# The last four steps of both output projections, instead of the last two, run block by block of tokens

## The reference

```
# first block
mix = concatenate([rmsnorm(o_a), rmsnorm(o_b)]) @ w_out          # first output projection
x = x + rmsnorm(mix, post_mix_g)
h = rmsnorm(x, pre_ffn_g)
u = causal_dwconv(h @ w_up, conv_w, conv_b); gate, val = split(u)
x = x + rmsnorm((gelu(gate) * val) @ w_down, post_ffn_g)
# second block, with shifts, scales and gates from a modulation network of c
x = x + g_a * (concatenate([attn, pool]) @ w_out_2)              # second output projection
hm = modulate(rms_norm(x, norm_mlp_w), sh_m, sc_m)
x = x + g_m * (square(relu(hm @ w_mlp_up)) @ w_mlp_down)
return rms_norm(x, final_norm_w)
```

## Time and profile before

| | |
|---|---|
| median of 3 runs | 2138.3 us (2136.77 to 2139.04) |
| profiled execution | 2135.51 us, its span 2133.8 us |
| mean granted TensorE clock | 0.996 of full |
| PE busy | 2100.0 us (98%) |
| DVE busy | 1552.3 us (73%) |
| ACT busy | 1091.9 us (51%) |

### The profile page before, as it was taken

One profiled execution on the slowest core, in us unless ns is written; L12 is line 12 of the kernel. 1 busy time (PEld: TensorE's weight loads), 2 busy tenths in 40 slices (PEclk: granted clock), 3 DMA queues, 4 the chain that ended last, 5 costly groups with the idle time before them and its releaser, 6 DMA issues.

```text
span 2133.8 us, 33198 instructions
## 1 busy us (share of the span) xinstructions
PE 2100.0 (98%) x10453; PEld 1750.3 (82%) x10453; DVE 1552.3 (73%) x2201; ACT 1091.9 (51%) x1499; POOL 120.3 (6%) x223
## 2 busy tenths in 40 slices
PE   6999999999999999999999999999999999999998
PEld 5888788888888888888888867888888888888886
DVE  4998889888988888768787554566656656655766
ACT  5445654655545554355587465464434434443444
POOL 1110000000001000100000000010000000000000
PEclk9999999999999999999999999999999999999999
DMA  9988168888899788987856542657667766766763
GB/s 342 305 287 268 60 227 266 271 271 283 276 305 302 264 277 297 296 261 247 258 176 197 182 138 100 188 172 253 208 197 233 221 192 225 237 193 213 226 208 109
DMA packets 282338, 492.35 MB, mean 231 GB/s; under 512 B 26385, under 2 KB 120849, under 8 KB 280657
## 3 DMA queue, kind: packets, MB, share of 16 engines
q1 hardware_dynamic: 251648, 373.52, 53.9%
q0 software_dynamic: 30256, 116.84, 16.5%
q10 hardware_dynamic: 288, 0.11, 0.0%
HBM read 488.24 MB, written 2.13 MB: 230 GB/s over the span
## 4 chain that ended last, share of the span: by engine, by line
PE 97%; ACT 1%; DVE 1%; issue 1%; SPq 0%; DMA 0%; ACTq 0%; DVEq 0%
PE G L1977 21%; PE G L1979 21%; PE G L1978 21%; PE G L1992 6%; PE T L1992 6%; PE T L1994 3%; PE G L1994 3%; PE T L1979 3%; PE T L1978 3%; PE T L1977 3%; PE T L2140 1%; PE T L2216 1%; PE T L2365 1%; PE T L2026 1%; PE G L2347 1%; PE G L2120 1%
## 5 line engine op out<-in xcount | busy, mean ns | idle before, releaser
L1135 DVE TENSOR_TENSOR w_lo<-raw,w_hi 128x1024 fp32r<-128x1024 f32 (+1 forms) x704 | 850.3, 1218 | 442.3 <-ACT w_hi L588 440.2
L588 ACT ACTIVATE w_hi<-raw 128x1024 fp32r<-128x1024 f32 (+1 forms) x704 | 740.9, 1055 | 810.9 <-PE G L1979 525.3
L1977 PE MATMUL G<-w_hi,h_both 128*128 128x512 f32 (+1 forms) x1144 | 448.4, 392 | 14.8 <-issue 8.5
L1979 PE MATMUL G<-w_hi,h_both 128*128 128x512 f32 (+1 forms) x1144 | 444.2, 388 | 0.0
L1978 PE MATMUL G<-w_lo,h_both 128*128 128x512 f32 (+1 forms) x1144 | 444.2, 388 | 0.0
L1977 PE MATMUL G<-w_hi,a_hi 128*128 128x512 f32 x880 | 344.8, 392 | 1.1 <-ACT pooled L1053 0.7
L1979 PE MATMUL G<-w_hi,a_lo 128*128 128x512 f32 x880 | 343.1, 390 | 0.0
L1978 PE MATMUL G<-w_lo,a_hi 128*128 128x512 f32 x880 | 343.0, 390 | 0.0
L1977 PEld LDWEIGHTS G<-w_hi,h_both 128*128 128x128 f32 x1144 | 215.8, 189 | 60.0 <-issue 15.7
L1979 PEld LDWEIGHTS G<-w_hi,h_both 128*128 128x128 f32 x1144 | 215.9, 189 | 44.2
L1978 PEld LDWEIGHTS G<-w_lo,h_both 128*128 128x128 f32 x1144 | 216.0, 189 | 42.2
(11 more groups left out here) (294 smaller groups left out, 2140.5 us busy)
## 6 DMA issues: line engine op xcount, KB each, us to landing
ada_w<-in_w_ada_turned POOLq DMA_DIRECT2D x192, 512.0 KB, 5.7
raw<-in_w_up SPq DMA_DIRECT2D x352, 256.0 KB, 4.8
raw<-in_w_mlp_up SPq DMA_DIRECT2D x256, 256.0 KB, 2.8
raw<-in_w_mlp_down SPq DMA_DIRECT2D x256, 256.0 KB, 3.3
raw<-in_w_in SPq DMA_DIRECT2D x224, 256.0 KB, 4.0
raw<-in_w_down SPq DMA_DIRECT2D x176, 256.0 KB, 4.9
raw<-in_w_out SPq DMA_DIRECT2D x128, 256.0 KB, 3.6
raw<-in_w_in SPq DMA_DIRECT2D x16, 136.0 KB, 3.3
```

The source lines that it names most:

```text
L588: act.activation(w_hi[:, s % 4, :, 0:width], raw[:, s % 8, :, 0:width], ACT.Copy).then_inc(hi_ready, 1)
L1135: dve.tensor_tensor(w_lo[:, s % 4, :, 0:width], raw[:, s % 8, :, 0:width], w_hi[:, s % 4, :, 0:width].bitcast(F32), ALU.subtract).then_inc ...
L1977: pe.matmul(out, ah, wh, start=f, stop=False)
L1979: mm = pe.matmul(out, al, wh, start=False, stop=l)
```

## The change

In both output projections, steps 28 to 31 go by `last_steps` (its argument `n` is 4 in place of the default 2), and `steps` ends after step 27. PE does steps 28 to 31 for block 0, 24 matmuls, and then steps 28 to 31 for block 1. The matmuls are the same ones, in another order. Nothing changes on ACT, DVE, POOL or SP.

```diff
@@ first output projection
-        steps(s0 + 24, 0, 6, 1, H, r, e0 + 4)
-        last_steps(s0 + 30, H[0], 12, r)
+        steps(s0 + 24, 0, 4, 1, H, r, e0 + 4)
+        last_steps(s0 + 28, H[0], 8, r, 4)
@@ second output projection
-        steps(s0 + 24, 0, 6, 1, A, r, e0 + 4)
-        last_steps(s0 + 30, A[0], 12, r)
+        steps(s0 + 24, 0, 4, 1, A, r, e0 + 4)
+        last_steps(s0 + 28, A[0], 8, r, 4)
```

## The result

The change made the kernel slower: 2143.93 us as the median of 12 runs (2140.75 to 2145.68), against 2137.94 us before (12 runs, 2136.65 to 2139.04). That is 6.0 us of medians; the ratio is 1.0028, with a 95% interval of 1.0019 to 1.0036. It lies in the stated range, 0.6 us from the stated 2143.3, and 0.28% is beyond the 0.2% that tells it from no change. The runs also spread over 4.9 us, where before they spread over 2.4.

What follows compares the result with a forecast made beforehand. PE, busy 98% of the span, was taken as the bound, with both paths starting at the unmoved last matmul. Delays of 2.95 + 1.58 us plus 0.5 us for the clock, on 2138.3, gave 2143.3 us; range 2139.9 to 2146.0.

Steps and rivals of the forecast that it cites:

- Block 0 has nothing to give: Both projections' ends: the path starts at the last matmul, which doesn't move, so the gain is bounded by 0.
- The delay of the first place: First projection's end: step 32's low part 4.08 us later on DVE, so block 1's reciprocal and PE's transposes 2.95 us later.
- The delay of the second place: Second projection's end: step 33's splits 2.72 us later, so `weighed` of block 1, fillers and transposes 1.58 us later.
- No stall within the block: PE, steps 28 to 31: step 31's weights are ready before their earlier use, so cost 0 in both projections.
- a sign of being wrong: A gap opening between the matmuls of steps 28 to 31 was named as showing the forecast wrong.
- The cover of 0.68 us: First projection: step 31's low part on DVE is ready 0.68 us before block 0's matmuls need it.
- The rival: PE stalls within the block: a late modulation tile delays step 31's low part, a 1.7 us stall, 2145.0 us; chance 0.08.
- The clock, 0.5 us: First projection: 3.09 us of PE idleness may drop the clock, costing 1.0 us at even chances, so 0.5 us.
- a fall in the second: Rival: the clock falls in both places or stays low longer, 3 us more, 2146.5 us; chance 0.07.
- The absorbed delay: Rival: PE's waits before the next layer's first matmul absorb 2.8 us, leaving 1.7 us, 2140.0 us; chance 0.25.
- Block 0's early finish: Rival: ACT and DVE take block 0 before step 33's weights, so nothing is late, 2138.3 us; chance 0.1.

Runs made afterwards that it cites:

- e4: The change, with ACT and DVE doing block 0's work before the splits of steps 32 and 33, and two first-place modulation tiles later: 2138.23 us, ratio 1.0002.
- e2: The kernel before, with only the second projection's last four steps run by blocks: 2139.80 us against 2137.61, ratio 1.0008.
- e1: The kernel before, with only the first projection's last four steps run by blocks: 2140.74 us against 2137.61, ratio 1.0014.
- e6: The change, with one modulation tile of DVE's first-place list moved behind the low part of step 31: 2145.54 us against 2137.71 before, ratio 1.0036.
- e11: The change itself, measured again: 2142.47 us against 2137.56 for the kernel before, ratio 1.0029.
- e12: The kernel of e6, measured again: 2143.11 us against 2137.56 for the kernel before, ratio 1.0028.
- e3: The change with three steps (29 to 31) instead of four by blocks in both projections: 2140.54 us against 2137.61 before, ratio 1.0013.
- e10: The change with no first-place fillers, and 40 second-place fillers instead of 27, not waiting for block 1's `weighed`: 2142.92 us against 2137.56 before, ratio 1.0029.

## Why the prediction was right, point by point

- **Block 0 has nothing to give.** Shown by e4: with block 0 used early, the times are those of before.
- **The delay of the first place, 2.95 us.** Measured 2.88 (2.28 to 5.16 from last matmul to transposes), 2.89 in the distance. The low part of step 32 starts at 361.30, and counted from the last matmul's start that is 2.50 us before it, instead of 362.80 - 356.22 = 6.58: 4.08 us later, as worked out.
- **The delay of the second place, 1.58 us.** Measured 1.58 to 1.60 in the change and in e2, the same with three steps.
- **No stall within the block, cost 0.** Held in three of five traces (within 0.1 us). In the change's own trace a gap of 0.70 us opened there, which the prediction had named as a sign of being wrong. The cover of 0.68 us was too thin to be counted on: it was read from one execution, and in another one a tile's data came 1.17 us late. The rival priced 1.7 us for a whole tile; what came was 0.3 and 0.7.
- **The clock, 0.5 us.** The mis-sized term. I took a fall in the first place as even, at 1.0 us, and gave a fall in the second no more than a part of 0.07. With 16 fillers the clock fell in the first place in four of five traces (e1, e6, e11, e12; not in the change's own). It stayed at 1.2 GHz for 6.8, 6.8, 3.4 and 6.8 us, which cost 2.39, 1.79, 0.43 and 2.39 us beyond the delay. In the second place, with the 27 fillers late, it fell in four of six (the change, e3, e6, e12; not e2, e11), for 3.4 us and at 1.6 to 1.7 us each. The mean of these is 1.4 + 1.1 = 2.5 us. The medians ask for less: the change and e11 lie 5.5 us over before on average, the two delays take 4.5 of it, and with the gap's 0.2 (1.0 over five traces) 0.8 is left for the clock. The granted clocks of all runs on record lie between. Their mean is 0.9952 for the change (12 runs) and 0.9951 for e11 (7), against 0.9964 for the kernel before (33). That is 0.0012 x 2142 / 0.5 = 5 us more at 1.2 GHz in an execution; in the eight falls above, 37.5 us at 1.2 GHz cost 13.7 us, and at that rate 5 us cost 1.8 us. This is an estimate, since the clocks are recorded to 0.001.

In the trace of before, the longest idle time between matmuls that left the clock up was 1.71 us, and those of 3.40 and 8.27 us brought it down; the 3.09 us lay between. My upper bound for one fall, 1.7 us for 3.4 us of work at half speed, was too low as well. That trace already held a fall of 6.8 us, within and behind the 8.27 us without a matmul; its stretches show where it began and ended:

```profile
50.00:51.00 1.00, 0.00 (x0) 0.00 (x0) 1.00 (x3) 0.00 (x0) 0.00 (x0) 0.58 0.94 354
...
56.00:57.00 1.00, 1.00 (x4) 0.71 (x4) 1.00 (x3) 0.00 (x0) 0.00 (x0) 0.50 0.97 266
57.00:58.00 1.00, 1.00 (x6) 0.83 (x5) 1.00 (x2) 0.00 (x0) 0.51 (x1) 1.00 1.00 358
```

The Trainium skill ("TensorE: Matmul & The Clock Gate", Part 1) says that the throttled clock is the default and activity lifts it. e10 agrees (0.50 from 366.70, after 3.6 us at nothing, and 1.00 again from 373.50, after PE had worked). The second place doesn't fit it as simply: in the change's trace the clock fell while transposes ran without a pause, 1.4 us after they had begun.

- **The rivals.** The absorbed delay (0.25) is out: the waits for h before the first matmul of the next layer are 1.13 and 1.72 us in the change, where they were 1.13 and 1.71. Only where transposes at 1.2 GHz took its place is the first of them shorter (0.29 to 0.77 us in e1, e6, e10, e11 and e12). Block 0's early finish (0.1) is out as the lists stand.
- **The size.** 5.0 forecast, 6.0 and 4.9 measured. It rests on two delays that hold to 0.1 us, on a stall put at 0 that came to 0 to 0.7, and on the clock, which comes out differently in each execution. That the time itself came within 0.6 us is in part luck: the loss was 1.0 us larger than stated, and the median of before, which the forecast was added to, came out 0.4 us lower in 12 runs than in 3.

## What to carry to other kernels

When the work of one step is held together by token block, ask first what is released late: here the slots of the last steps' weights came free 12 and 18 matmuls later, and in the hand-written lists of ACT and DVE the refill of those slots stood ahead of the very work that was to start early. An order changed on one engine needs the others' lists changed with it (e4), and even then it gives only what lies on the path, which here began at the last matmul. A gap on PE costs more than its length where it brings the clock down: in e1 a wait of 3.02 us was followed by another 2.39 us of loss.

## What of the hardware was not expected

The clock fell while PE was busy: in the change's second place 1.4 us after 27 back-to-back transposes had begun, with 2.37 us of idleness before them; they took 4.79 us instead of 3.17. In e3 and e12 it fell 1.3 and 1.0 us after they had begun, in e6 as they began. The same gap, and the same fillers, left it at 2.4 GHz in e2 and e11. What decides between the two, no run here shows. A fall can cost between 0.43 us (e11, 3.4 us at 1.2 GHz) and 2.39 us (e1, 6.8 us) at one and the same place.
